# Stationary tiles that step by four columns in the delta and gate stages of a one-core float32 block stack, and 51 products behind the last one

## What is computed

```python
h = rmsnorm(x, g_pre[i])
proj = h @ w_in[i]
qkv, z_a, b_raw, a_raw, glu_in, z_b, gate_logits = jnp.split(proj, _split_points(), axis=-1)
qkv = jax.nn.silu(causal_depthwise_conv(qkv, w_conv_qkv[i]))
o_a = gated_delta_chunked(q, k, v, g_log, beta)
y_a = (rmsnorm(o_a, g_dn_out[i]).reshape(B, S, DN_WIDTH) * jax.nn.silu(z_a)) @ w_br_a[i]
u = causal_depthwise_conv(jax.nn.glu(glu_in, axis=-1), w_dw[i]) + b_dw[i]
y_b = (jax.nn.silu(layernorm(u, ln_g[i], ln_b[i])) * jax.nn.silu(z_b)) @ w_br_b[i]
```

## Time and profile before

| what | value |
|---|---|
| median of 2 runs | 2704.07 us (2703.56 to 2704.59) |
| the profiled execution, its own time | 2705.86 us |
| its span, from the first to the last instruction | 2704.2 us |
| mean granted TensorE clock | 0.996 of full speed |
| PE, share of the span busy | 99% |
| weight loads (PEld) | 86% |
| DVE, ACT, POOL | 63%, 46%, 6% |
| DMA | 183 GB/s on average |

### The profile page before, as it was taken

The page is one execution under the profiler, slowest core; times in us unless marked ns, Lnnn a source line. Parts: engine busy times, 40 slices in busy tenths (PEclk is TensorE's granted clock), DMA queues, the critical chain, the costliest instruction groups (busy, mean ns, idle before and its releaser), DMA issues.

```text
span 2704.2 us, 38890 instructions
## 1 busy us (share of the span) xinstructions
PE 2666.8 (99%) x14738; PEld 2318.4 (86%) x14738; DVE 1703.4 (63%) x2260; ACT 1235.5 (46%) x1477; POOL 161.2 (6%) x331
## 2 busy tenths in 40 slices
PE   8999999999999999999989999999999999999997
PEld 7888888888888888888879999999998999878886
DVE  5555555554555554555456676675889898776564
ACT  5444444444444444444445545454434444364453
POOL 0000000000000000000001240422000000000000
PEclk9999999999999999999999999999999999999999
DMA  7555555555555555555544555545555555455654
GB/s 250 179 179 179 179 179 175 175 186 187 194 190 189 191 193 188 192 192 203 195 159 156 165 174 155 188 154 166 185 187 195 183 193 191 154 194 191 225 177 139
DMA packets 150030, 495.36 MB, mean 183 GB/s; under 512 B 28496, under 2 KB 29232, under 8 KB 149360
## 3 DMA queue, kind: packets, MB, share of 16 engines
q1 hardware_dynamic: 147376, 482.25, 54.0%
q0 software_dynamic: 2496, 10.87, 1.3%
HBM read 489.89 MB, written 3.16 MB: 182 GB/s over the span
## 4 chain that ended last, share of the span: by engine, by line
PE 95%; DVE 2%; DMA 1%; ACT 1%; issue 0%; SPq 0%; POOL 0%; POOLq 0%; DVEq 0%; ACTq 0%
PE PS L1521 23%; PE PS L1523 23%; PE PS L1522 23%; PE PS L1535 6%; PE PS L1537 6%; PE PS L1538 6%; PE PS L1697 2%; PE PS L1546 1%; DMA raw<-in_stream 1%; PE PS L1704 1%; ACT whi L531 0%; DVE wlo L902 0%; PE PS L1713 0%; PE PS L1591 0%; PE PS L1597 0%
## 5 line engine op out<-in xcount | busy, mean ns | idle before, releaser
L902 DVE TENSOR_TENSOR wlo<-raw,whi 128x1024 fp32r<-128x1024 f32 x900 | 1100.5, 1226 | 948.2 <-ACT whi L531 942.7
L531 ACT CAST whi<-raw 128x1024 fp32r<-128x1024 f32 x900 | 941.3, 1048 | 1363.2 <-PE PS L1523 1023.5
L1521 PE MATMUL PS<-whi,aH 128*128 128x512 f32 x1792 | 702.5, 392 | 4.2 <-DVE wlo L902 1.8
L1522 PE MATMUL PS<-wlo,aH 128*128 128x512 f32 x1792 | 698.1, 390 | 0.0
L1523 PE MATMUL PS<-whi,aL 128*128 128x512 f32 x1792 | 698.0, 390 | 0.0
L1535 PE MATMUL PS<-aH,whi 128*128 128x256 f32 x1536 | 439.6, 286 | 0.1
L1537 PE MATMUL PS<-aL,whi 128*128 128x256 f32 x1536 | 434.8, 283 | 0.0
L1538 PE MATMUL PS<-aH,wlo 128*128 128x256 f32 x1536 | 434.6, 283 | 0.0
L1521 PEld LDWEIGHTS PS<-whi,aH 128*128 128x128 f32 x1792 | 336.9, 188 | 74.7 <-DVE wlo L902 3.1
L1523 PEld LDWEIGHTS PS<-whi,aL 128*128 128x128 f32 x1792 | 336.7, 188 | 70.4
L1522 PEld LDWEIGHTS PS<-wlo,aH 128*128 128x128 f32 x1792 | 337.0, 188 | 68.2
(11 more groups left out here) (292 smaller groups left out, 2180.7 us busy)
## 6 DMA issues: line engine op xcount, KB each, us to landing
raw<-in_stream SPq DMA_DIRECT2D x900, 512.0 KB, 3.3
H<-in_x SPq DMA_DIRECT2D x4, 512.0 KB, 7.9
pB<-in_pool_b POOLq DMA_DIRECT2D x4, 512.0 KB, 3.9
iT<-diag_in SPq DMA_DIRECT2D x16, 128.0 KB, 2.7
bg<-in_b_gate POOLq DMA_DIRECT2D x8, 256.0 KB, 4.1
out<-eb SPq DMA_DIRECT2D x4, 512.0 KB, 2.9
dmask<-in_dmask POOLq DMA_DIRECT2D x1, 1536.0 KB, 11.0
dT<-cum_rows SPq DMA_DIRECT2D x6, 256.0 KB, 4.4
```

Of the source, the lines that this page charges most:

```text
L531: nc.scalar.copy(whi[:, s], raw[:, s]).then_inc(hi_done, 1)
L902: nc.vector.tensor_tensor(wlo[:, s], raw[:, s], whi[:, s].bitcast(F32), ALU.subtract).then_inc(lo_done, 1)
L1521: mm(out, hi[:, kt + k, tok], whi[:, s, k], start=kt + k == 0, stop=False)
L1522: mm(out, hi[:, kt + k, tok], wlo[:, s, k], start=False, stop=False)
```

## The change

It has three parts. On the host, chunks() gets an argument woven: in a woven chunk the 512 columns are reordered so that column m * 4 + c holds what was column c * 128 + m. stream() asks for it in the blocks that chunk_b reads. On the chip, chunk_b takes its stationary tile c as the columns c, c + 4, c + 8 and so on of the chunk, 128 of them, from whi and from wlo. So each tile holds the same values as before, at a step of four columns of float32. And behind the last chunk PE gets 51 products on banks 4 to 7, of which nothing reads the results: with stationary tiles of steps 1, 2 and 4, a moving operand of two stretches, one of step 2, tiles of 64 columns or 64 partitions, another offset, and five with 256 moving columns.

```diff
                 for k in range(KPC):
+                    high, low = (v[:, s, k].rearrange("p (m c) -> p c m", c=QT) for v in (whi, wlo))
                     for c in range(QT):
-                        w = slice(c * P, (c + 1) * P)
                         end = last and k == KPC - 1
-                        mm(half(bank, c), whi[:, s, k, w], aH[:, kt + k], start=kt + k == 0 and c % 2 == 0, stop=False,
+                        mm(half(bank, c), high[:, c], aH[:, kt + k], start=kt + k == 0 and c % 2 == 0, stop=False,
                            skip_group_check=True)
-                        mm(half(bank, c), whi[:, s, k, w], aL[:, kt + k], start=False, stop=False, skip_group_check=True)
-                        ins = mm(half(bank, c), wlo[:, s, k, w], aH[:, kt + k], start=False, stop=end,
+                        mm(half(bank, c), high[:, c], aL[:, kt + k], start=False, stop=False, skip_group_check=True)
+                        ins = mm(half(bank, c), low[:, c], aH[:, kt + k], start=False, stop=end,
                                  skip_group_check=True)
...
+            spare, flat_w = aH[:].rearrange("p k n -> p (k n)"), whi[:].rearrange("p s k n -> p (s k n)")
+            for n in range(5):
+                mm(PS[:, 4], spare[:, 0:P], flat_w[:, 0:NB], start=n == 0, stop=n == 4)
+            for n in range(6):
+                mm(PS[:, 4 + n % 2], spare[:, 0:P], flat_w[:, 0:NB], start=n < 2, stop=n > 3)
+            for n in range(5):
+                mm(PS[:, 4], spare[:, 0:2 * P:2], flat_w[:, 0:NB], start=n == 0, stop=n == 4)
+            for n in range(5):
+                mm(PS[:, 5], spare[:, 0:4 * P:4], flat_w[:, 0:NB], start=n == 0, stop=n == 4)
+            for n in range(5):
+                mm(PS[:, 6].rearrange("p (a n) -> p a n", a=2), flat_w[:, 0:P], aH[:, 0:4:2], start=n == 0, stop=n == 4)
+            for n in range(5):
+                mm(PS[:, 7], spare[:, 0:P], flat_w[:, 0:2 * NB:2], start=n == 0, stop=n == 4)
+            for n in range(5):
+                mm(PS[0:64, 4], spare[:, 0:64], flat_w[:, 0:NB], start=n == 0, stop=n == 4)
+            for n in range(5):
+                mm(PS[:, 5], spare[0:64, 0:P], flat_w[0:64, 0:NB], start=n == 0, stop=n == 4)
+            for n in range(5):
+                mm(PS[:, 6], spare[:, 96:96 + P], flat_w[:, 96:96 + NB], start=n == 0, stop=n == 4)
+            for n in range(5):
+                mm(PS[:, 7, 0:SEQ], spare[:, 0:P], flat_w[:, 0:SEQ], start=n == 0, stop=n == 4)
...
-def chunks(w, columns):
+def chunks(w, columns, woven=False):
...
+        if woven:
+            block = block.reshape(-1, QT, P).transpose(0, 2, 1).reshape(-1, NB)
...
-        out += chunks(w, [DM + n, n, 2 * DM + n, z_a + n])
+        out += chunks(w, [DM + n, n, 2 * DM + n], True) + chunks(w, [z_a + n])
     for n in whole:
-        out += chunks(w, [glu + n, glu + DM + n, z_b + n, gate + n]) + chunks(a["w_br_a_2"][0], [n])
+        out += chunks(w, [glu + n, glu + DM + n, z_b + n], True) + chunks(w, [gate + n]) + chunks(a["w_br_a_2"][0], [n])
```

## The result

The changed kernel takes 3227.03 us (median of 2 runs, 3226.41 to 3227.65) against 2704.07 us: the ratio is 1.1934, with a 95% interval of 1.1911 to 1.1958. That is 523 us slower. The direction and the place were forecast; the size was not: 3156 us was predicted with 3200 us as the upper end, so the measured time lies 27 us outside of the range.

A forecast was written before the change was run, and what follows sets the result against it. The prediction took TensorE (PE), busy 99%, as the bound, with the distance between product starts deciding. It added 452 us for 4608 stepped loads and 0 us for host and tail to 2704 us: 3156 us, range 2699 to 3200 us.

The forecast's parts named there:

- The bound, the count and the cover: PE bounds the kernel; 4608 chunk_b products stand 0.120 us apart, their loads need 0.107 to 0.112 us, cover 8 ns.
- Host, ACT, DVE, DMA: Weaving before launch, and the copies and subtraction on contiguous rows as before: 0 us, both bounds 0.
- The 51 products: Behind the last product, 11.0 us of PE work hidden under the tail with 3.5 us of cover left: cost 0 us.
- the moving step of two: In the tail, five products that might take twice as long: 1.1 us more, still inside the cover.
- The price of the stepped load: chunk_b's step-four loads take 213 ns, plus 5 ns: distance 0.218 us instead of 0.120 us, cost 452 us.
- double price: chunk_b's stepped loads take 213 ns, distance 0.218 us, 452 us more, 3156 us; chance 0.45.
- The mechanism behind that number: chunk_b loads travel no faster than chunk_a's moving stream, four columns in 1.67 ns, so 213 ns a load.
- "Free": Rival for chunk_b loads: the step costs nothing and the load stays hidden, 2704 us; chance 0.35 with no step on chip.
- The part price: Rival for chunk_b loads: less than double, say 0.160 us, 184 us more, 2888 us; chance 0.12.
- Paying for every skipped column: Rival for chunk_b: loads of 0.428 us, up to 1419 us more, 4123 us; chance 0.05 with anything over 3200 us.
- the gain: Rival for chunk_b: the new read order removes 0.013 us a product, 60 us, giving 2644 us; chance 0.03.

The follow-up runs named there:

- the table: Unchanged kernel plus tail rows of ten products at various stationary and moving steps, two fp32r runs: 2711.39 us against 2703.3 us, 2715.78 us against 2703.62 us.
- the rows "alone": Tail rows behind the unchanged kernel with 64 moving columns, so the load decides: 112, 118, 174, 233 ns for stationary steps 1 to 4.
- the table with narrow products: Unchanged kernel plus twelve tail rows of ten products, with 64 or 512 moving columns at several stationary steps, and two 256-column rows; only distances counted.

## Why the prediction was wrong, point by point

*The bound, the count and the cover: right.* PE's distance between starts decided, 4608 products carried the change, and 522.3 us of the 523 us lie in their stretch. The load's own time with contiguous columns, 0.112 us, was read from the small products of the earlier trace rows and came out at 112 ns in the table, so the cover of 8 ns was real.

*Host, ACT, DVE, DMA: right.* DVE's and ACT's busy times moved by under 2 us, and none of these ends a wait of PE that wasn't there before. ACT's wait for free buffers grew instead: before L531 it stood 328.9 us for L1538, now 850.0 us.

```profile
ACT whi L531 <- PE PS L1538: 850.0, 191, 6.3
```

*The 51 products: right in price, short in length.* Forecast 0 us, measured a ratio of 0.9998. With their latency they took 12.9 us, where the forecast had them from 2689.4 to 2700.7, 11.3 us. Of the difference 1.1 us is the moving step of two, as the forecast had bounded it: (2.44 - 0.63) / 4 = 0.45 us a product from the first row below (0.63 us is the record of one). The second row is the one with stationary step two: (1.33 - 0.39) / 4 = 0.235 us. The forecast had said that steps two and four under 512 columns would not show in the starts; they do, by some 7 ns.

```profile
3217.14 2.44 PE L1968 MATMUL PS<-whi,aH 128*128 128x512 f32 x5
3213.66 1.33 PE L1962 MATMUL PS<-whi,aH 128*128 128x512 f32 x5
```

*The price of the stepped load: the step that failed.* The forecast put it at "with the 5 ns by which 0.112 exceeds 0.107 the distance becomes 0.218 us". Measured are 0.233 us. The 213 ns for the columns may be right, since step three and step four differ by 60 ns as 160 and 213 nearly do, but what comes on top of them is 20 ns and not 5: the rows "alone" exceed 107, 107, 160 and 213 ns by 5, 11, 14 and 20 ns. Fifteen ns missing, times 4608, are about 70 us, and 3156 + 70 = 3226 us. What that fixed part is, no run shows. The record of the load was off the same way: 192 to 330 ns, 138 ns more where about 100 were named. The upper end of 3200 us was too near for the same reason: it took 0.227 us as the longest for double price, though nothing in the rows bounded the fixed part of a slow load.

*The mechanism behind that number: wrong.* The forecast took the pace at which the moving stream travels over a stretch as the ceiling of the load. At a step of four that gives the same 213 ns as an account by pieces, so the changed kernel couldn't tell them apart, and that the forecast came within 71 us with it was luck. Steps of eight and sixteen can: 0.240 us in the full kernel and 0.220 us in the table, where travel would have needed about 0.44 and 0.87 us. What the runs show is a price that is reached when each column stands 16 bytes from the next, and that then no longer grows. The Trainium skill, Advanced Engine Details and Errata, section SBUF Cachelines, has lines of 16 bytes and wants two hits on each. For fp32r stationary tiles the trace agrees: step two (two hits) 0.118 us, step three 0.173 us, steps four to sixteen (one hit) 0.220 to 0.247 us. For the moving operand it doesn't: a step of two, still two hits on a line, already doubles the distance from 0.120 to 0.228 us, and four and eight add nothing. The measurement decides there. For bf16 stationary tiles, hidden at every step, no run shows it.

*The rivals.* "Free" falls for step four and is right for step two under 256 moving columns. The part price falls for step four as well, and is what step three has. Paying for every skipped column is refuted by the change itself, 0.233 us where it asked for 0.428 us; the gain by the change and by step two, which saved nothing.

## What to carry to other kernels

A stationary tile has its own time, and it costs nothing only while that stays under the product directly ahead of it; 128 fp32r columns take 0.112 us in a row, 0.118 us at step two, 0.174 us at step three and 0.22 to 0.25 us at step four and beyond, against 0.120 us of a product with 256 moving columns. So keep stationary columns in a row, or at most every second one, where products are narrow, and don't step the moving operand of fp32r where PE is the limit: a step of two doubled the distance under 256 and under 512 columns. When a row of the profile doesn't show an access, bound its fixed part as well as its part per column, and ask at which other size two explanations with the same number would part.

## What the runs showed of the hardware that was not expected

The pace of a load at step four or eight doesn't follow the granted clock of the products. In the table with narrow products the clock fell at 2691.3, in the row with 64 moving columns and step four, and rose again at 2701.5. Before it fell PE had done products of 64 columns for 4 us. The table by stretch of that run, the rest of the rows with steps four to sixteen first, then the row with 512 moving columns and step one:

```profile
2691.30:2697.70 6.40, 6.40 (x29) 6.40 (x29) 5.54 (x9) 0.00 (x0) 1.58 (x2) 0.50 0.37 139
2697.72:2701.50 3.78, 3.78 (x11) 3.00 (x11) 0.67 (x2) 0.00 (x0) 0.00 (x0) 0.50 0.85 318
```

At a granted clock of 0.50, the lower level of 1.2 GHz, loads of step four stood 0.233 us apart as they do at full clock, while the 512-column products took 0.427 us instead of 0.227 us. That row is therefore not in the table above, and its cell is taken from L1958 of the changed kernel. The changed kernel shows the same in its stepped stretch, where the clock fell a few times for 3 to 7 us; one such stretch, and products inside it, five in 1.17 us:

```profile
1477.70:1484.50 6.80, 6.80 (x31) 6.58 (x30) 3.38 (x9) 2.32 (x2) 0.00 (x0) 0.50 0.22 80
```

```profile
1479.71 0.43 PE L1538 MATMUL PS<-aH,wlo 128*128 128x256 f32 x1
...
1480.88 0.43 PE L1537 MATMUL PS<-aL,whi 128*128 128x256 f32 x1
```

So these dips cost the stepped products nothing. It isn't so for contiguous tiles. The transposes L1546 load 128 columns in a row and stream 128. In the kernel before, eight of them at full clock and sixteen at the lower one:

```profile
868.13 1.03 PE L1546 MATMUL PS<-con,mz 128*128 128x128 f32 x8
1398.14 3.68 PE L1546 MATMUL PS<-con,XS 128*128 128x128 f32 x16 [8.22 <-DVE XS L1109]
```

```profile
1394.00:1403.30 9.30, 5.03 (x22) 4.63 (x23) 6.70 (x15) 4.17 (x9) 5.81 (x11) 0.50 0.38 99
```

With records of 0.27 and 0.42 us for one, that is (1.03 - 0.27) / 7 = 0.109 us and (3.68 - 0.42) / 15 = 0.217 us: the distance doubles with the clock. The 128 moving columns alone would explain an estimated 0.107 us at the lower level (twice half of the 0.107 us that 256 columns cost at full clock), so it is the contiguous load that got slower here, unless a transpose streams otherwise than a product, which no run excludes. At the lower clock, then, a step of four would cost little over a contiguous tile: products of chunk_b in the kernel before stood 0.213 us apart there (three in 0.64 us), against 0.233 us.

```profile
1402.54 0.41 PE L1538 MATMUL PS<-aH,wlo 128*128 128x256 f32 x1
...
1403.18 0.41 PE L1538 MATMUL PS<-aH,wlo 128*128 128x256 f32 x1
```

The distance at steps of four and more isn't constant: 227 ns at step five, 233 to 236 at four, 238 to 247 at eight, 220 to 222 at sixteen. No run here says what separates them.
